# Head norms of the first mixer: the inverse root as a power on GpSimd

## What is computed

```
def rmsnorm(x, g):
    y = xf * lax.rsqrt(jnp.mean(xf * xf, axis=-1, keepdims=True) + EPS)      # EPS = 1e-6
    return y * g

q = rmsnorm(q.reshape(b, l, 8, 128), g_q)       # 8 query heads of width 128
k = rmsnorm(k.reshape(b, l, 4, 128), g_k)       # 4 key heads of width 128
ki = rmsnorm(ki, g_kidx)                        # one index key of width 64
y_att = dsa_attention(q, k, v, qi, ki, wi)      # 64 keys are picked by an index score, then softmax
```

## Time and profile before

| | |
|---|---|
| median of 3 runs | 2675.21 us (2672.89 to 2678.63) |
| the profiled execution, its own time | 2677.62 us |
| its span, first to last instruction | 2675.8 us |
| TensorE busy | 2642.0 us (99%) |
| VectorE busy | 1741.5 us (65%) |
| ScalarE busy | 1322.5 us (49%) |
| GpSimd busy | 208.0 us (8%) |
| mean granted TensorE clock | 0.995 |

### The profile page before, as it was taken

One profiled execution on the slowest core, in us unless ns is written; L12 is line 12 of the kernel. 1 busy time (PEld: TensorE's weight loads), 2 busy tenths in 40 slices (PEclk: granted clock), 3 DMA queues, 4 the chain that ended last, 5 costly groups with the idle time before them and its releaser, 6 DMA issues. The chain is left out here.

```text
span 2675.8 us, 35946 instructions
## 1 busy us (share of the span) xinstructions
PE 2642.0 (99%) x14484; PEld 2274.5 (85%) x14484; DVE 1741.5 (65%) x2361; ACT 1322.5 (49%) x1903; POOL 208.0 (8%) x182
## 2 busy tenths in 40 slices
PE   9999999999999999999999999999999999999998
PEld 8778888888888888888889888988888888888887
DVE  7888796555556555785776767566665555565555
ACT  6545455535445344565554545455555354454454
POOL 3014001000000000140411300000000000000000
PEclk9999999999999999999999999999999999999999
DMA  7644445555555555566333333355555555555553
GB/s 269 165 166 158 164 167 189 189 191 186 198 181 189 203 186 194 186 251 241 142 133 137 125 127 113 131 198 189 189 197 186 198 188 191 189 189 193 185 200 130
DMA packets 68174, 481.91 MB, mean 180 GB/s; under 512 B 8008, under 2 KB 8136, under 8 KB 11177
## 3 DMA queue, kind: packets, MB, share of 16 engines
q1 hardware_dynamic: 65520, 467.43, 48.8%
q0 software_dynamic: 1968, 10.75, 1.5%
q10 hardware_dynamic: 520, 1.43, 0.1%
HBM read 473.29 MB, written 6.29 MB: 179 GB/s over the span
## 5 line engine op out<-in xcount | busy, mean ns | idle before, releaser
L1262 DVE TENSOR_TENSOR w_lo<-weight_ring,w_hi 128x1024 fp32r<-128x1024 f32 x882 | 1083.2, 1238 | 697.8 <-ACT w_hi L2115 696.7
L2115 ACT CAST w_hi<-weight_ring 128x1024 fp32r<-128x1024 f32 x884 | 916.4, 1048 | 646.0 <-PE bank L545 408.9
L533 PE MATMUL bank<-h,w_hi 128*128 128x512 f32 x2848 | 906.9, 400 | 0.0
L536 PEld LDWEIGHTS bank<-h,w_lo 128*128 128x128 f32 x2848 | 535.9, 188 | 126.6
L533 PE MATMUL bank<-mix,w_hi 128*128 128x512 f32 x1776 | 569.8, 402 | 4.1 <-DVE w_lo L1262 1.9
L536 PE MATMUL bank<-h,w_lo 128*128 128x256 f32 x2848 | 560.8, 278 | 0.0
L533 PEld LDWEIGHTS bank<-h,w_hi 128*128 128x128 f32 x2848 | 437.2, 189 | 7.7 <-issue 5.7
L543 PE MATMUL bank<-w_hi,mix 128*128 128x512 f32 x1056 | 411.2, 389 | 0.0
L544 PE MATMUL bank<-w_lo,mix 128*128 128x512 f32 x1056 | 410.9, 389 | 0.0
L545 PE MATMUL bank<-w_hi,mix 128*128 128x512 f32 x1056 | 410.8, 389 | 0.0
L536 PEld LDWEIGHTS bank<-mix,w_lo 128*128 128x128 f32 x1776 | 335.2, 189 | 79.3
(11 more groups left out here) (369 smaller groups left out, 1758.9 us busy)
## 6 DMA issues: line engine op xcount, KB each, us to landing
weight_ring<-in_w_up SPq DMA_DIRECT2D x128, 1024.0 KB, 4.8
weight_ring<-in_w_down SPq DMA_DIRECT2D x128, 1024.0 KB, 4.8
weight_ring<-in_w_merge SPq DMA_DIRECT2D x32, 1024.0 KB, 4.8
weight_ring<-in_w_gdn SPq DMA_DIRECT2D x24, 1024.0 KB, 4.8
weight_ring<-in_w_papb SPq DMA_DIRECT2D x16, 1024.0 KB, 4.8
weight_ring<-in_w_o SPq DMA_DIRECT2D x16, 1024.0 KB, 4.8
weight_ring<-in_w_xbc SPq DMA_DIRECT2D x12, 1024.0 KB, 4.8
weight_ring<-in_w_q SPq DMA_DIRECT2D x8, 1024.0 KB, 4.8
```

Source lines behind the costliest of these rows:

```text
L533: e.matmul(bank[:, :], w_hi[:, unit_at % UNITS, o + j * P:o + (j + 1) * P], x[:, :, at + j * S:at + (j + 1) * S], start=first and j == 0, ...
L536: done = e.matmul(bank[:, 0:S], w_lo[:, unit_at % UNITS, o + j * P:o + (j + 1) * P], x[:, 0, at + j * S:at + (j + 1) * S], start=False, st ...
L1262: e.tensor_tensor(w_lo[:, i, :], ring[:, p % PIECES, half * UNIT:(half + 1) * UNIT], w_hi[:, i, :].bitcast(F32), ALU.subtract).then_inc(un ...
L2115: e.copy(w_hi[:, i, :], ring[:, p % PIECES, half * UNIT:(half + 1) * UNIT]).then_inc(unit_hi, 1)
```

## The change

ScalarE's two `Sqrt` activations become `Identity` with the same scale and bias, so `root_1` holds the mean plus EPS. GpSimd then raises it to the power -0.5, by a tensor-tensor operation against a column of -0.5 that is broadcast along the free axis. VectorE's seven reciprocals go; its multiplications wait for the same semaphore `head_inv`, which GpSimd now raises. The column of -0.5 is a third column of `eps`, set by one more memset at the start. GpSimd does step 0 behind the layer's norm and the other six behind the halving of the taps, ahead of the convolutions.

```diff
-        eps = sb("eps", [P, 2])
+        eps = sb("eps", [P, 3])
...
             def head_norms():                                  # VectorE
                 yield from rounds(1)
-                e.wait_ge(head_root, 1)
-                e.reciprocal(root_1[:, 0:S], root_1[:, 0:S]).then_inc(head_inv, 1)
                 e.wait_ge(head_inv, 1)
...
-                    e.wait_ge(head_root, s + 1)
-                    e.reciprocal(root_1, root_1).then_inc(head_inv, 1)
                     e.wait_ge(head_inv, s + 1)
                     e.scalar_tensor_tensor(out=dst, in0=dst, scalar=gain, in1=root_1, op0=ALU.mult,
...
             def head_norms():                                  # ScalarE
-                e.activation(root_1[:, 0:S], psum[6][:, 0:S], ACT.Sqrt, bias=eps[:, 0:1],
+                e.activation(root_1[:, 0:S], psum[6][:, 0:S], ACT.Identity, bias=eps[:, 0:1],
                              scale=1.0 / IDX_DIM).then_inc(head_root, 1)
...
-                    e.activation(root_1, psum[6][:, :], ACT.Sqrt, bias=eps[:, 0:1], scale=1.0 / P).then_inc(head_root, 1)
+                    e.activation(root_1, psum[6][:, :], ACT.Identity, bias=eps[:, 0:1], scale=1.0 / P).then_inc(head_root, 1)
...
         def _(e):                                              # GpSimd
             e.memset(eps[:, 1:2], EPS * P * EPS).then_inc(ones_set, 1)
+            e.memset(eps[:, 2:3], -0.5).then_inc(half_set, 1)
...
             gather(0)
             normed(0, root_1[:, 0:S])
+            def head_inverse(s):
+
+                n = S if s == 0 else 2 * S
+                e.wait_ge(head_root, s + 1)
+                e.tensor_tensor(root_1[:, 0:n], root_1[:, 0:n], eps[:, 2:3].to_broadcast([P, n]), ALU.pow).then_inc(head_inv, 1)
+
+            e.wait_ge(half_set, 1)
+            head_inverse(0)
             e.wait_ge(rows_copied, 1)
             e.dma_start(bias_spread, rows.unsqueeze(1).to_broadcast([NSA_HEADS, P, 2 * S])).then_inc(rows_written, 16)
             e.wait_ge(vecs_loaded, 16)
             halve_convolutions()
+            for s in range(1, 7):
+                head_inverse(s)
```

More of the change, by code:

```diff
@@ L458, in build @@
         assert len(unit_of) == UNIT_AT["end"]
-        ones_set = sem("ones_set")
+        ones_set, half_set = sem("ones_set"), sem("minus_half_set")
         vecs_loaded, params_loaded = sem("vecs_loaded"), sem("params_loaded")
```

## The result

The changed kernel takes 3184.67 us, the median of 4 runs (3181.84 to 3188.35), against 2674.05 us before: a ratio of 1.190, 95% interval 1.189 to 1.192. It is 511 us slower. The prediction was 2693 us with a range to 2790; it had the direction and missed the size by a factor of 28.

A forecast was written before the change was run, and what follows sets the result against it. TensorE bounds the kernel, VectorE close behind and the bound in the stage's last third. At p = 7 the steps cost 15 us, step 0 1, the clock 2: 2675.2 + 18 = 2693 us, range 2670 to 2790.

The forecast's parts named there:

- I take p = 7: p is the time in us of one GpSimd power over 128x512, taken as 7 from VectorE's reciprocal-to-multiplication ratio of 4.5.
- the upper end: Highest price considered for a GpSimd power: some 30 elementary steps, each a pass of 1.5 us, p = 45.
- What bounds the stage: In the changed stage TensorE sets the pace, VectorE is close behind and bounds the last third; reserve 0.7 to 0.9 us.
- The slope: Beyond break-even prices of 3.3 to 4.8 us, each further us of p costs TensorE 1 us in each of six steps.
- The sum for p = 7: Whole loss at that price: 15 us for steps 1 to 6, +1 for step 0, +2 for the clock, +18 us.
- The two counts: Loss in steps 1 to 6: 17.0 us step by step, 13.0 us by VectorE's own work; 15 was taken.
- Step 0: Half-width power of 3.5 us ends up to 1.8 us later than the reciprocal; first index score still finds its keys; +1 us.
- the clock: TensorE's new waits of 2 to 4 us bring falls to the lower clock, partly hidden: +2 us.
- The gain for a cheap operation: Rival A, p up to 3.3: TensorE's waits and lower clock in the stage go, 4.5 us, outer end 7; chance 0.22.
- The table load at nothing: ScalarE's table load of 1.28 us, which goes, was costed at nothing; only step 1's root is ready sooner, 86.5 against 87.8.
- The power begins behind a `w_lo` in flight: GpSimd's power and VectorE's w_lo exclude each other; otherwise powers of steps 1, 4, 6 start 0.8 to 1.0 us sooner.
- For step 5: Power begins at 142.7, w_lo and a sum take 1.5 us, no reserve: p may be 4.0 us; loss 3.0 us.

The follow-up runs named there:

- e1_mult: The changed kernel with a multiplication in place of GpSimd's power, every wait kept: 2668.05 us, ratio 0.9976.
- e8_p4: The changed kernel with the power over only 25 of 512 columns (13 of 256 in step 0), a power of 4.3 us: 2677.41 us, ratio 1.0005.
- e9_p7: The changed kernel with the power over only 42 of 512 columns (21 in step 0), a power of 7.0 us: 2696.84 us, ratio 1.0077.
- e4_noroot: The kernel before with Identity in place of Sqrt in the head norms, VectorE's reciprocals kept: 2677.20 us, ratio 1.0005.

## Why the prediction was wrong

The step that failed is the price of a power, "I take p = 7", with its bounds of 1.5 and 45 us. It measures 82 us, beyond the upper bound; with a multiplication in its place (e1_mult) the whole loss is gone. Both ways of getting at it failed. That a hard operation stands to a plain one on GpSimd as on VectorE (4.5) was an analogy with nothing behind it: the factor is 79 against a multiplication alone (1.04 us), and 48 to 55 against the 1.5 to 1.7 us of rows 9. And the upper end, 30 elementary steps as passes of 1.5 us each, passed for a bound, but counted the arithmetic of a method that I had assumed. The range then went only to p = 23; 0.15 was left above, for a quantity of which no row said anything.

Given that price, the way to the time held in the main. Point by point:
- What bounds the stage. VectorE close behind TensorE, with a reserve of about 1 us in a step: the time of e8_p4, with a power of 4.3 us, is that of before.
- The slope, 1 us in each of six steps: 6.1 in all from 12 to 82 us. With the measured price the steps give 6 x 82.05 - 25.0 = 467 us and step 0 gives 37, 505 in all; TensorE's waits grew by 492. The 13 us too many and the 18.2 us of lower clock nearly offset each other, and so 505 comes close to the measured 511.
- The sum for p = 7: +18 us forecast, +20.2 measured in e9_p7 against the runs beside it. The two counts gave 17 and 13 for the six steps, and I took 15; the waits grew by 13.4, so the lower count was right. Step 0 was put at 1 and measured 1.5, the clock at 2 and measured 5.8. That the sum comes out so close is in part luck.
- Step 0: TensorE's wait is 37.4 us, one power of 41.75 less the reciprocal of 1.75, which leaves 2.6 us of reserve. The prediction gave no figure for it; that a power of 3.5 us does not delay the keys fits e9_p7, where one of 4.3 does not.
- The gain for a cheap operation: 4.5 us forecast with 7 as outer end, 7.1 measured, of which the trace has 5.7 in the stage.
- The table load at nothing: e4_noroot shows no gain.
- The power begins behind a `w_lo` in flight: shown by the 0.8 us in e9_p7. For step 5 I had taken 1.5 us off for a `w_lo` and a sum between root and multiplication. That was wrong: in e9_p7 the power there starts with no `w_lo` in flight and takes 7.05 us, and TensorE's wait is 3.7 instead of 1.80 us, so that 5.2 us would break even and not 4.0.
- The clock: +2 us at p = 7 was too little, it cost 5.8 us in e9_p7; in the changed kernel it is 18.2 us, with TensorE idle for most of each step and at a granted clock of 0.57 to 0.59.

## What to carry to other kernels

An operation that no trace shows has no price by analogy: measure it alone, at two widths, before it goes onto an engine that others wait for. When one engine's multiplication waits in the queue in which also the weights are made, each microsecond beyond its reserve is paid by TensorE, once for every step. A sum that comes out right can hide terms that are off in both directions; the waits and TensorE's busy time in the trace tell them apart. The gain of such a move is bounded beforehand by the waits that can go, here 7 us; a price that can cost 500 has to be known first.

## What the runs showed of the hardware that was not expected

- GpSimd's power of two inputs: 0.159 us for each column plus 0.3 to 0.4 us, 81.9 us for 512, the same for the five exponents, the constant and varied values and the numbers of partitions (1 to 128) that were tried.
- Beside a power of 82 us on GpSimd, a subtraction on VectorE that starts 0.15 us after it takes 0.74 us longer (0.10 us with 128 columns, nothing with 64), and the next one is as short as ever.
- TensorE can wait three times, for 1.9 to 3.2 us, and keep a granted clock of 1.00 (e9_p7, steps 2 to 4), while a wait of 1.80 us before was followed by 0.57 for 4 us. What tells the two apart was not found.
- Logarithm and exponential with a table load ahead of each, 3.9 us on ScalarE, are cheaper here than a reciprocal of 3.35 us on VectorE, because ScalarE had the room and VectorE had not.
